# Transposes of a two-layer encoder spread over the last four matmuls of a unit

## The reference

```python
for l in range(DEPTH):                      # DEPTH = 2
    h = rmsnorm(x, norm1_g[l])              # x: (1, 256, 2048)
    proj = h @ w_in[l]                      # 2048 x 4352
    aq, ak, av, bq, bk, bv, cq, ck, cv = jnp.split(proj, splits, axis=-1)
    out_a = mixer_chunked_relbias(...)      # 8 heads, bias by distance
    out_b = mixer_swa_sinks(...)            # 16 query heads, 2 kv heads, rotary, sinks
    out_c = mixer_diff(...)                 # 4 heads, difference of two softmax maps, rotary
    x = x + jnp.concatenate([out_a, out_b, out_c], axis=-1) @ w_out[l]   # 2048 x 2048
    h2 = rmsnorm(x, norm2_g[l])
    x = x + jnp.square(jax.nn.relu(h2 @ w_up[l])) @ w_down[l]            # 2048 x 8192 x 2048
```

## Time and profile before

| | us |
|---|---|
| median of three executions | 2070.12 |
| the profiled execution | 2069.04 |
| its span, first to last instruction | 2067.1 |
| TensorE matmuls busy in the span | 2061.8 (100%) |
| VectorE busy | 1267.3 (61%) |
| ScalarE busy | 990.7 (48%) |
| GpSimd busy | 191.7 (9%) |
| mean share of the DMA queue of the weight loads | 61.9% of 16 engines |

### The profile page before, as it was taken

The page is one execution under the profiler, slowest core; times in us unless marked ns, Lnnn a source line. Parts: engine busy times, 40 slices in busy tenths (PEclk is TensorE's granted clock), DMA queues, the critical chain, the costliest instruction groups (busy, mean ns, idle before and its releaser), DMA issues.

```text
span 2067.1 us, 26774 instructions
## 1 busy us (share of the span) xinstructions
PE 2061.8 (100%) x10762; PEld 1733.5 (84%) x10762; DVE 1267.3 (61%) x1646; ACT 990.7 (48%) x1328; POOL 191.7 (9%) x196
## 2 busy tenths in 40 slices
PE   9999999999999999999999999999999999999999
PEld 7887788888888888888888877888888888888887
DVE  7767566655565556556677775665655655665664
ACT  6557644443443444344455586444434434434442
POOL 6253100000000000001023531000000000000000
PEclk9999999999999999999999999999999999999999
DMA  9477866666666666666665689666666666666663
GB/s 301 136 229 194 225 184 184 191 191 192 189 192 194 187 190 193 193 185 193 183 178 148 205 203 242 176 183 190 192 192 190 192 194 187 191 193 192 186 193 122
DMA packets 207451, 396.64 MB, mean 192 GB/s; under 512 B 13674, under 2 KB 22352, under 8 KB 207328
## 3 DMA queue, kind: packets, MB, share of 16 engines
q1 hardware_dynamic: 202640, 379.52, 61.9%
q0 software_dynamic: 4512, 15.33, 4.0%
q10 hardware_dynamic: 176, 0.09, 0.0%
HBM read 377.95 MB, written 2.12 MB: 184 GB/s over the span
## 4 chain that ended last, share of the span: by engine, by line
PE 99%; DMA 0%; SPq 0%; DVE 0%; issue 0%
PE psum L496 40%; PE psum L516 23%; PE psum L500 20%; PE psum L519 12%; PE psum L531 1%; PE psum L603 1%; PE psum L582 0%; PE psum L628 0%; PE psum L590 0%; PE psum L588 0%; DMA x<-in_x_dram 0%; PE psum L638 0%; PE psum L619 0%; PE psum L620 0%; PE psum L618 0%; PE psum L640 0%
## 5 line engine op out<-in xcount | busy, mean ns | idle before, releaser
L894 DVE TENSOR_TENSOR w_lo<-raw_ring,w_hi 128x1024 fp32r<-128x1024 f32 (+1 forms) x692 | 850.9, 1231 | 680.8 <-ACT w_hi L715 679.4
L715 ACT CAST w_hi<-raw_ring 128x1024 fp32r<-128x1024 f32 (+1 forms) x720 | 749.7, 1042 | 995.3 <-PE psum L500 604.1
L516 PE MATMUL psum<-xt,w_hi 128*128 128x512 f32 x2048 | 512.9, 392 | 0.0
L496 PE MATMUL psum<-w_hi,ht_hi 128*128 128x512 f32 x1280 | 501.8, 392 | 0.0
L496 PE MATMUL psum<-w_hi,ht_lo 128*128 128x512 f32 x1280 | 498.6, 390 | 0.0
L516 PEld LDWEIGHTS psum<-xt,w_hi 128*128 128x128 f32 x2048 | 368.8, 189 | 66.3
L500 PE MATMUL psum<-w_lo,ht_hi 128*128 128x512 f32 x1280 | 342.5, 389 | 0.0
L519 PEld LDWEIGHTS psum<-xt,w_lo 128*128 128x128 f32 x2048 | 279.4, 190 | 19.9
L519 PE MATMUL psum<-xt,w_lo 128*128 128x256 f32 x2048 | 285.6, 282 | 0.0
L500 PEld LDWEIGHTS psum<-w_lo,ht_hi 128*128 128x128 f32 x1280 | 240.3, 188 | 50.3
L496 PEld LDWEIGHTS psum<-w_hi,ht_hi 128*128 128x128 f32 x1280 | 240.4, 188 | 49.6 <-issue 1.0
(11 more groups left out here) (144 smaller groups left out, 968.2 us busy)
## 6 DMA issues: line engine op xcount, KB each, us to landing
raw_ring<-in_w_up_dram SPq DMA_DIRECT2D x256, 512.0 KB, 3.7
raw_ring<-in_w_down_dram SPq DMA_DIRECT2D x256, 512.0 KB, 3.7
raw_ring<-in_w_in_dram SPq DMA_DIRECT2D x128, 512.0 KB, 4.7
raw_ring<-in_w_out_dram SPq DMA_DIRECT2D x64, 512.0 KB, 4.8
w_lo<-raw_ring POOLq DMA_DIRECT2D x28, 512.0 KB, 5.8
raw_ring<-in_w_in_dram SPq DMA_DIRECT2D x16, 256.0 KB, 2.8
x<-in_x_dram SPq DMA_DIRECT2D x8, 256.0 KB, 7.5
out_dram<-x SPq DMA_DIRECT2D x3, 512.0 KB, 2.7
```

The costliest lines, as they stand in the source:

```text
L496: pe.matmul(bank[r][:, 0:cols], t[:, kt, r * P:(r + 1) * P], w_hi[:, slot, j, 0:cols], start=first and j == 0 and n == 0, stop=False, skip ...
L516: pe.matmul(bank[:, f, :], w_hi[:, w, j, f * P:(f + 1) * P], both, start=kt == 0, stop=False, skip_group_check=True)
L715: act.copy(w_hi[:, u % AHEAD, :, 0:cols], raw_ring[:, u % RAWS, :, 0:cols]).then_inc(hi_ready, 1)
L894: dve.tensor_tensor(w_lo[:, u % AHEAD, :, 0:cols], raw_ring[:, u % RAWS, :, 0:cols], w_hi[:, u % AHEAD, :, 0:cols].bitcast(F32), ALU.subtr ...
```

## The change

`rows_unit` gets a parameter `between`. Where a group of transposes belongs to a row unit, the group's waits are made behind the first of the last four matmuls, and each of the four transposes is issued behind one of these four. `unit_done` is raised by the fourth matmul as before, `t_ready` by the fourth transpose. The group no longer follows the scores, value products and probability transposes of its unit, it precedes them. Groups behind up units stay as they are.

```diff
-            def rows_unit(pl, u, src, kts, chunk, first, last, cols):
+            def rows_unit(pl, u, src, kts, chunk, first, last, cols, between=None):
...
-                    for j, kt, r in group:
+                    for n, (j, kt, r) in enumerate(group):
                         mm = pe.matmul(bank[r][:, 0:cols], src[0][:, kt, r * P:(r + 1) * P], w_lo[:, slot, j, 0:cols],
                                        start=False, stop=last and j == 1, skip_group_check=True)
+                        if between is not None:
+                            if n == 0:
+                                t_may_start(pl, between)
+                            blocks = blocks_of(between)
+                            if n == 3:
+                                mm.then_inc(unit_done, 1)
+                            t = pe.transpose(ps_t[:, n * P:(n + 1) * P], blocks[n], ident)
+                            if n == 3:
+                                t.then_inc(t_ready, 1)
+                                return
...
+            def t_may_start(pl, s):
+                use = T_USE[s]
+                if use[0] == "qk":
                     pe.wait_ge(normed, pl.at(len(NORMS), NORMS.index(use[1:]) + 1))
...
                 pe.wait_ge(t_free, pl.at(T_USES, T_BEFORE + T_NUMBER[s]))
                 pe.wait_ge(pv_copied, pl.at(MIXES, 1 + sum(v <= s for v in VALUES)))
-                transposes(blocks)
+
+            def use_t(pl, s):
+                t_may_start(pl, s)
+                transposes(blocks_of(s))
...
                 if s in PROBS_T:
                     transpose_probs(pl, PROBS_T[s])
-                if s in T_USE:
-                    use_t(pl, s)
...
-                if s in T_USE and used(pl, s):
+                if part == "up" and s in T_USE and used(pl, s):
                     use_t(pl, s)
```

More of the change, by code:

```diff
@@ L535, in x_panel, with blocks_of @@
                 return [x[:, r, kt * P:(kt + 1) * P] for kt in (2 * k, 2 * k + 1) for r in range(RT)]
-            def use_t(pl, s):
+            def blocks_of(s):
                 use = T_USE[s]
                 if use[0] == "qk":
-                    c = use[1]
+                    if use[1] == 3:
+                        return [head_sq[:, r * SEQ + g * P:r * SEQ + (g + 1) * P] for g in range(2) for r in range(RT)]
+                    return [head_in[:, use[2] * CW + b * P:use[2] * CW + (b + 1) * P] for b in range(4)]
+                if use[0] == "mixC":
+                    k = use[1]
+                    return [mixed[:, r, b * P:(b + 1) * P] for b in (2 * (k - 6), 2 * (k - 6) + 1) for r in range(RT)]
+                return x_panel(use[1])
+            def t_may_start(pl, s):
+                use = T_USE[s]
+                if use[0] == "qk":
                     pe.wait_ge(normed, pl.at(len(NORMS), NORMS.index(use[1:]) + 1))
[L542 to L545, removed]
                 elif use[0] == "mixC":
-                    k = use[1]
                     pe.wait_ge(mix_ready, pl.l + 1)
-                    blocks = [mixed[:, r, b * P:(b + 1) * P] for b in (2 * (k - 6), 2 * (k - 6) + 1) for r in range(RT)]
                 else:
@@ L557, in use_t @@
                         pe.wait_ge(evicted[n % 2], Place(pl.l).evictions(n) + 1)
-                    blocks = x_panel(use[1])
                 pe.wait_ge(t_free, pl.at(T_USES, T_BEFORE + T_NUMBER[s]))
                 pe.wait_ge(pv_copied, pl.at(MIXES, 1 + sum(v <= s for v in VALUES)))
-                transposes(blocks)
+            def use_t(pl, s):
+                t_may_start(pl, s)
+                transposes(blocks_of(s))
             def scores(pl, n):
@@ L644, in mix @@
                 chunk, k, cols = proj_or_out(s)
+                between = s if s in T_USE else None
                 if s < PU:
@@ L647, in mix @@
                         pe.wait_ge(panel_done, pl.at(PANELS, k + 1))
-                    rows_unit(pl, s, xt, (2 * k, 2 * k + 1), chunk, k == 0, k == UPC - 1, cols)
+                    rows_unit(pl, s, xt, (2 * k, 2 * k + 1), chunk, k == 0, k == UPC - 1, cols, between)
                 else:
@@ L653, in mix @@
                         pe.wait_ge(pv_copied, pl.at(MIXES, (2 * k + 1 if k >= 2 else 2 * k + 13) + 2))
-                    rows_unit(pl, s, ht, (2 * k, 2 * k + 1), chunk, k == PAIRS_CB[0], k == PAIRS_A[1], cols)
+                    rows_unit(pl, s, ht, (2 * k, 2 * k + 1), chunk, k == PAIRS_CB[0], k == PAIRS_A[1], cols, between)
                 if pl.l == 0 and s < 3:
@@ L684, in mlp @@
                         pe.wait_ge(h_done, pl.at(H_CHUNKS, done, 4))
-                    rows_unit(pl, s, ht, (8 * buf + 2 * k, 8 * buf + 2 * k + 1), n, k == 0, k == 3, CW)
-                if s in T_USE and used(pl, s):
+                    rows_unit(pl, s, ht, (8 * buf + 2 * k, 8 * buf + 2 * k + 1), n, k == 0, k == 3, CW,
+                              s if s in T_USE and used(pl, s) else None)
+                if part == "up" and s in T_USE and used(pl, s):
                     use_t(pl, s)
```

## The result

| | before | after |
|---|---|---|
| median, us (20 runs each) | 2069.73 | 2073.85 |
| lowest and highest | 2068.84 to 2071.39 | 2073.14 to 2075.77 |
| profiled execution | 2069.04 | 2073.76 |
| its span | 2067.1 | 2071.7 |

The ratio of after to before is 1.002, with a 95% interval of 1.0013 to 1.0027. The change makes the kernel 4.1 us slower, 0.2%.

What follows compares the result with a forecast made beforehand. TensorE was taken to bound the kernel, busy 2061.8 of 2067.1 us. Profiled 2069.04 plus 1.6 interleaving plus 3.6 stalls gave 2074.2; against the median 2070.12, 2075.3 us (+0.25%), range 2070.8 to 2079 for 8 in 10.

Steps and rivals of the forecast that it cites:

- No gain from the interleaving: TensorE's transposes: each still costs 0.11 us between long matmuls, the load behind it exposed; rival of hidden loads 0.08.
- The price of the interleaving: Four interruptions per group for one: 0.035 us more in each of 53 groups, 1.9 us, less units 3 to 5, 1.6.
- fixed part: Cost of each interruption of TensorE's matmuls beyond the transpose's 0.11: 0.03 to 0.04 us, spread over about seven matmuls.
- The stalls, 3.6 us: TensorE waits reached too early at units 23, 24, 65, 57, 55 and two near the edge; bounds 0 and about 5.
- Unit 65: Transpose waits for `pv_copied` from L1063, late by 0.67: stall 0.60 us, in both layers 1.20.
- Unit 24: Waits for L776 to empty the bank, 0.31 late through the later `unit_done`: stall 0.35 us, in both layers 0.70.
- Unit 57: Waits for L1063, late by 0.48 including 0.35 from unit 55's signal: stall 0.41 less 0.03 drift, both layers 0.76 us.
- groups near the edge: Two other groups whose releases come within 0.05 us of too late: 0.1 us together.
- Unit 23: Layer 0 alone: the norm L989 ends 0.43 us behind the first L500, stall 0.36 us.
- its own formula: Stall at a group: release less start of the first L500, plus 0.05 plus 0.11 less 0.23: lateness less 0.07 us.
- Unit 55, 0.44 us: L500 already waits 0.14 for the adding DMA, issued later through unit 47's signal: 0.22 us more per layer, both 0.44.
- border to slower: Whole kernel: a change of about 0.2%, 4.1 us, can be told from none, so slower begins at 2074.3 us.

Runs made afterwards that it cites:

- e2: Kernel before with only the groups of units 14, 23, 24, 57 and 65 interleaved, the other 43 behind their unit: 2072.07 us, ratio 1.0011.
- e4: Changed kernel with only a group's waits behind the first of the last four matmuls, the four transposes behind the unit as before: 2074.11 us, ratio 1.0022.
- e12: e4 run once more, unchanged, for another look at unit 55: 2074.05 us.
- e6: e4 with the low parts of units 55 and 57 made by VectorE instead of the adding DMA: 2076.39 us, ratio 1.0032.
- e7: Kernel before with units 55 and 57 split by VectorE instead of the adding DMA: 2075.17 us, ratio 1.0025.
- e1: Changed kernel with the groups of units 14, 23, 24, 57 and 65 put back behind their unit: 2070.28 us, ratio 1.0004.
- e8: Changed kernel with units 55 and 57 split by VectorE instead of the adding DMA: 2078.44 us, ratio 1.0043.
- early block: Changed kernel with all four transposes of a group in one block behind the first of the last four matmuls: 2076.49 us, ratio 1.0032.
- e10: Kernel before with each transpose of 47 groups issued twice, eight in one block: 2089.03 us, 19.5 over before.

## Why the prediction held, by its steps

**No gain from the interleaving: right.** This rested on a single instruction, L659, and on the step that a transpose is bound by the load behind it. The price held: 0.35 from transpose to transpose, and 0.116 for each of 188 lone ones. The reason fits the rows, in which the weights of the next L500 start to load with the transpose and not before it (78.29 both, 78.63 both at unit 23), but no run changed the length of that load, so it is argued.

**The price of the interleaving, 0.035 a group: too high.** It was 0.020 in 37 undisturbed groups, so 53 of them make 1.1 us and not 1.6 to 1.9. As the prediction had it, the one matmul that follows doesn't pay the whole fixed part behind an interruption.

**The stalls, 3.6 us: right in kind at the four units named, and right in sum partly by luck.** Measured were 3.5: 0.44 too much was forecast at unit 55, and 0.4 too little at units 23 and 14. Unit 65: 0.60 forecast per layer, 0.63 measured (0.65 less the interleaving). Unit 24: 0.35 forecast, 0.29. Unit 57: 0.38 forecast, 0.40 and 0.43, with 0.3 of it from unit 55's signal, as e2 and e4 show; the forecast took its drift of 0.03 off twice, and without that slip it is 0.41. ScalarE's L715 started later by the 0.35 forecast (1.39 behind the first weight load of unit 15's w_lo matmuls before, 1.74 after, and the same at units 39, 46 and 47). Unit 14 was counted among groups near the edge and cost 0.24 in one profile and nothing in another.

**Unit 23: 0.36 forecast, 0.64 measured, with a cause left out.** The norm is late by 0.76 (77.84 against 77.08), not 0.43, and that isn't chance. The chain that ended last in the changed kernel shows where it comes from (start us, us, what; L970 is the old L954, L775 the old L759):

```profile
55.84 0.25 PE psum L500
...
56.16 1.05 ACT w_hi L731
...
59.31 0.72 ACT head_in L775
...
60.05 1.23 DVE small L970
...
77.23 0.61 DVE head_in L1005
77.89 0.33 PE psum L508
```

The first row is the last L500 of unit 15, which has a group too. Its signal to ScalarE is 0.35 late, the evictions and the sum of the squares behind it are as late (L970 starts 5.63 behind unit 15's first w_lo weight load, 5.28 before), and from there to L1005 the chain is work of VectorE and ScalarE with none of TensorE in it. Nothing takes the delay up, and the norm eight units on is 0.35 late as well. The profiles divide by this. In six in which unit 15's signal isn't late (before, e2, e4, its repetition e12, e6 and e7) the norm ends 0.65 to 0.70 us behind unit 23's first w_lo weight load; in the changed kernel, e1 and e8 it is 0.98 to 1.05, and in the early block, whose signals are later still, 1.15. Unit 23 cost 0.38 to 0.40 in e2, e4, e12 and e6, 0.66 and 0.72 in the changed kernel and e8, and 0.81 in the early block. The prediction charged this very path at unit 57, for unit 55's group, but not at unit 23 for unit 15's. With it, its own formula gives 0.69.

**Unit 55, 0.44 us: wrong.** The step was to take 4.46 against 4.32 for a wait on the adding DMA. It wasn't one: the row of L500 there has no idle time, and the 0.14 lie at the scores behind the value product. The distance from unit 54's L500 to unit 55's, for which the forecast had 4.7, was 4.41 after the change. Nor did the later signal delay the DMA. Measured from the weight load of unit 47's first L500 (142.13 before, 143.34 after), L970, the old L954, starts at 5.63 where it was 5.28, but the DMA is issued at 22.53 (22.55 before). The delay is gone already in GpSimd's rotary work. Its timeline in the kernel before, layer 0:

```profile
152.76 1.81 POOL L1309 TENSOR_TENSOR head_sq<-head_in,rope_s 128x256 f32<-128x256 f32 x1
154.53 0.73 POOL L1310 TENSOR_TENSOR head_sq<-head_in,rope_s 128x256 f32<-128x256 f32 x1
```

And in the changed kernel:

```profile
154.32 1.45 POOL L1325 TENSOR_TENSOR head_sq<-head_in,rope_s 128x256 f32<-128x256 f32 x1
155.73 0.73 POOL L1326 TENSOR_TENSOR head_sq<-head_in,rope_s 128x256 f32<-128x256 f32 x1
```

The old L1309, the first of these, began 10.64 behind that load and took 1.81; here it begins 10.98 behind it and takes 1.45, so that both end 12.4 behind it. GpSimd's operation took up the delay. In the early block it starts later still, 11.10 behind, takes 1.32 and ends at 12.42.

**The size.** 5.2 us were forecast on the median and 4.1 measured (interval 2.7 to 5.6). In the two profiled executions 5.2 stand against 4.6: unit 55 and the interleaving were forecast about 1 us too high, units 23 and 14 0.4 too low. The other half of a microsecond is where the profiled executions lie among their runs. The forecast put its border to slower at 2074.3 and more weight on a slower kernel than that (0.53) than on about the same time (0.40). 2073.85 lies just below the border, although the interval is clear of no change.

## What to carry to other kernels

An instruction moved earlier carries its waits with it: before such a move, compare the end of each releaser with the place of the new wait, at each of the places. Ten of 53 places made 3.7 of 4.6 us here. A signal behind moved work is late by that work. Follow it to its end: it made the very next group's wait late at unit 24, that of two units on at unit 57, and that of eight units on, by way of ScalarE and VectorE, at unit 23, while at unit 55 it was taken up. Interleaving the short matmuls with long ones gained nothing here; a lone one cost 0.116 us where one in a block cost 0.108.

## What the runs showed of the hardware that I had not expected

- GpSimd took up a delay of 0.35 us without passing it on. An operation of it took 1.45 us and not 1.81, and 1.32 where it started 0.46 later. VectorE's L1044 ran beside it at the same time in all three. Why the end stays in place is open.
- The adding DMA of 512 KB landed after 4.5 to 10.3 us over all profiles. At unit 55, where it is alone but for its successor, it took 4.6 or 4.7 in sixteen of 22 cases, and 5.2 to 6.8 in the six with a 16 KB packet of the instruction queue between issue and landing. In these six 15 of its last 16 small packets were on time.
- After a block of four transposes the next ten or so 512-column matmuls start 0.225 to 0.235 apart in place of 0.227 (the kernel before). After a block of eight only the next three do so, 0.232 to 0.234 (e10). A pair of a lone transpose and a matmul took 0.344. What causes this stays open.
